# Two low-part subtractions per input projection of the first block move from VectorE to GpSimd

## The reference, cut to what matters

```python
hn = rms_norm(x, ln1)
proj = hn @ w_in                     # 1024 x 2824: the input projection
mq, mk, mv, sq, sk, sv, xqk, xv, xo, xi, xf = jnp.split(proj, idx, axis=-1)
mq, mk, sq, sk = (apply_rope(rms_norm(heads(a), g), cos, sin) for a, g in ...)
y_moba = moba_attention(mq, mk, mv)  # 6 heads, causal
qk = silu(causal_depthwise_conv(xqk, conv_w, conv_b))
h = mlstm_chunkwise(lq, lk, xv, i_pre, f_pre) * sigmoid(xo)   # 4 heads
y_swa = swa_attention(sq, sk, sv, sinks)   # 6 query heads, window 128
x = x + concat([y_moba, rms_norm(h), y_swa]) @ w_out
x = x + square(relu(rms_norm(x, ln2) @ w_up)) @ w_down
```

## Time and profile before

| | us |
|---|---|
| median of 3 runs | 1953.29 |
| lowest and highest | 1945.13, 1953.79 |
| the profiled execution, its own time | 1953.22 |
| its span | 1951.4 |
| PE busy in the span | 1851.1 (95%) |
| DVE busy | 1107.3 (57%) |
| ACT busy | 881.6 (45%) |
| GpSimd busy | 37.2 (2%) |
| the 274 splits on DVE (line 1013), sum and mean | 621.6, 2.276 |

### The profile page before, as it was taken

The page is one execution under the profiler, slowest core; times in us unless marked ns, Lnnn a source line. Parts: engine busy times, 40 slices in busy tenths (PEclk is TensorE's granted clock), DMA queues, the critical chain, the costliest instruction groups (busy, mean ns, idle before and its releaser), DMA issues.

```text
span 1951.4 us, 26268 instructions
## 1 busy us (share of the span) xinstructions
PE 1851.1 (95%) x11234; PEld 1593.2 (82%) x11234; DVE 1107.3 (57%) x1202; ACT 881.6 (45%) x1148; POOL 37.2 (2%) x29
## 2 busy tenths in 40 slices
PE   7898999989899999998999998998999999989998
PEld 6767999776799988776999986877999877868997
DVE  4865555485555555465655654556555654665554
ACT  5454444345444444434544543425444544344442
POOL 0000000000000000000000000000000000000000
PEclk9998999999899999999999998999999999998999
DMA  7463565645456574447555543366665652364552
GB/s 238 146 219 117 187 194 184 206 151 187 159 194 189 181 252 157 135 156 269 173 182 185 185 161 108 108 222 211 193 187 180 216 173 86 126 220 130 187 182 85
DMA packets 228235, 342.48 MB, mean 176 GB/s; under 512 B 9908, under 2 KB 118808, under 8 KB 227992
## 3 DMA queue, kind: packets, MB, share of 16 engines
q1 hardware_dynamic: 226928, 339.45, 53.6%
q10 hardware_dynamic: 1192, 1.36, 0.2%
HBM read 339.74 MB, written 1.05 MB: 175 GB/s over the span
## 4 chain that ended last, share of the span: by engine, by line
PE 89%; DVE 6%; ACT 3%; issue 1%; POOL 1%; ACTq 0%; DVEq 0%; POOLq 0%
PE PS L1604 16%; PE PS L1606 16%; PE PS L1605 16%; PE PS L1644 9%; PE PS L1645 9%; PE PS L1646 9%; PE PS L2032 2%; DVE LO L1013 1%; PE PS L1563 1%; PE PS L2013 1%; PE PS L2022 1%; PE PS L1941 1%; PE PS L1687 1%; POOL RS L565 1%; PE PS L2051 1%
## 5 line engine op out<-in xcount | busy, mean ns | idle before, releaser
L1013 DVE TENSOR_TENSOR LO<-RAW,HI 128x2048 fp32r<-128x2048 f32 (+1 forms) x274 | 621.6, 2276 | 447.5 <-ACT HI L584 446.9
L584 ACT CAST HI<-RAW 128x2048 fp32r<-128x2048 f32 (+1 forms) x274 | 516.7, 1894 | 321.3 <-PE PS L1606 257.3
L1644 PE MATMUL PS<-AH,HI 128*128 128x256 f32 x1424 | 408.4, 287 | 0.4 <-issue 0.4
L1645 PE MATMUL PS<-AL,HI 128*128 128x256 f32 x1424 | 405.8, 285 | 0.0
L1646 PE MATMUL PS<-AH,LO 128*128 128x256 f32 x1424 | 405.6, 285 | 0.0
L1604 PE MATMUL PS<-HI,AH 128*128 128x512 f32 (+2 forms) x848 | 318.1, 375 | 13.3 <-DVE MOD L1365 7.8
L1605 PE MATMUL PS<-LO,AH 128*128 128x512 f32 (+2 forms) x848 | 310.2, 366 | 0.0
L1606 PE MATMUL PS<-HI,AL 128*128 128x512 f32 (+2 forms) x848 | 310.0, 366 | 0.0
L1644 PEld LDWEIGHTS PS<-AH,HI 128*128 128x128 f32 x1424 | 276.6, 194 | 2.9 <-issue 2.3
L1645 PEld LDWEIGHTS PS<-AL,HI 128*128 128x128 f32 x1424 | 276.4, 194 | 1.6 <-issue 1.0
L1646 PEld LDWEIGHTS PS<-AH,LO 128*128 128x128 f32 x1424 | 276.2, 194 | 0.0
(11 more groups left out here) (244 smaller groups left out, 1640.2 us busy)
## 6 DMA issues: line engine op xcount, KB each, us to landing
RAW<-in_w_ff SPq DMA_DIRECT2D x96, 1024.0 KB, 5.4
RAW<-in_w_in SPq DMA_DIRECT2D x80, 1024.0 KB, 5.1
RAW<-in_w_mod SPq DMA_DIRECT2D x48, 1024.0 KB, 5.1
RAW<-in_w_up SPq DMA_DIRECT2D x32, 1024.0 KB, 5.5
RAW<-in_w_down SPq DMA_DIRECT2D x32, 1024.0 KB, 5.0
RAW<-in_w_o SPq DMA_DIRECT2D x12, 1024.0 KB, 6.1
RAW<-in_w_out SPq DMA_DIRECT2D x8, 1024.0 KB, 5.6
RAW<-in_w_attn_out SPq DMA_DIRECT2D x6, 1024.0 KB, 5.0
```

The lines of the kernel that those rows point to most:

```text
L584: return nc.scalar.copy(dst, src)
L1013: tt(LO[:, c % RAW_N, 0:n], RAW[:, c % RAW_N, 0:n], HI[:, NTH[c] % HL_N, 0:n].bitcast(F32), ALU.subtract).then_inc(s_lo, 1)
L1644: mm(o, wh, ah[:, j, :], start=j == 0, stop=False)
L1645: mm(o, wh, al[:, j, :], start=False, stop=False)
```

## The change

GpSimd takes over the subtraction of chunk 7 and of chunk 8 in both layers of the first block, four chunks in all, and counts them on a semaphore of its own, s_plo. In GpSimd's list they stand behind the second power of the layer (24 wide). DVE leaves these four out and numbers its own by LOW_NTH. `arrived(c)` waits for s_plo at these four chunks and for s_lo at the others.

```diff
+POOL_LOW = [k.c_in + j for k in LAYERS for j in (7, 8)]
+LOW_NTH = {c: i for i, c in enumerate(c for c in SPLITS if c not in POOL_LOW)}
...
+        s_plo = sem("chunk_split_by_pool")
...
                 for j, width in enumerate((2, 24, 2 * (NQK - 12), 8, 2)):
                     rsqrt(5 * l + j, width)
+                    if j == 1:
+                        for c in POOL_LOW[2 * l:2 * l + 2]:
+                            pool.wait_ge(s_hi, NTH[c] + 1)
+                            nc.gpsimd.tensor_tensor(LO[:, c % RAW_N, :], RAW[:, c % RAW_N, :],
+                                                    HI[:, NTH[c] % HL_N, :].bitcast(F32),
+                                                    ALU.subtract).then_inc(s_plo, 1)
...
             def ahead(c):
-                if c + SPLIT_LEAD in NTH:
+                if c + SPLIT_LEAD in LOW_NTH:
                     split(c + SPLIT_LEAD)
...
             def arrived(c):
-                pe.wait_ge(s_lo, NTH[c] + 1)
+                if c in POOL_LOW:
+                    pe.wait_ge(s_plo, POOL_LOW.index(c) + 1)
+                else:
+                    pe.wait_ge(s_lo, LOW_NTH[c] + 1)
```

## The result

The changed kernel takes 1976.05 us (median of 4 runs, 1966.39 to 1977.41) against 1953.54 of the kernel before (4 runs, 1945.13 to 1953.81): a ratio of 1.0115, 95% interval 1.0094 to 1.0135. It is slower by 22.5 us; 1978 was forecast, from 1970 to 1988. One of the four runs, at 1966.39, lies under that range. The profiled execution took 1977.2 us with a span of 1975.4, 24.0 more than before.

The account below looks back on a forecast made before the run. PE, busy 95% of the span, was taken as the bound, so its waits count. Per layer 11.6 us of late scores plus 0.9 for a second clock fall make 25.0 over two layers: 1953.2 + 25.0 = 1978 us, range 1970 to 1988.

Parts of the forecast that it names:

- The chain before the new work: Up to GpSimd's power, waits run through ACT's cast and DVE's split of chunk 9; power stays at 71.08 us.
- the value of 0 for the freed time: DVE's freed 4.6 us a layer gain nothing, since chunk 9's split waits for ACT's cast; upper end 4.6 us a layer.
- GpSimd's subtraction: One 128 x 2048 subtraction on GpSimd takes 4.9 us, taken as three passes at the pace of a memset.
- a sign that it is wrong: GpSimd's subtraction lasting under 2.5 or over 6 us would show the prediction wrong.
- PE's pause and start: PE idles 14.0 us ahead of chunk 7 in layer 0, waiting for GpSimd, and starts it at 80.25 us.
- The slow clock behind it: After the long pause PE runs chunk 7 partly at half clock, losing 2.6 us.
- The way to the scores: Chunk 11's split 1.99 us after its cast, mLSTM scores 3.49 us after the split: 94.05 against 82.43, 11.6 us late.
- The second fall of the clock: A later 3.1 us PE pause may lower the clock again, costing 0 to 2.6 us; a third, 0.9, was taken.
- The rival of engines in each other's way: DVE's scaling, 1.76 and 1.83 us, holds GpSimd's subtraction of chunk 7 by 3.6 us a layer: 1985 us; chance 0.20.
- what is added: Prediction's step on GpSimd's new work: wait for high parts free, each subtraction 4.9 us.
- The subtractions in time: Rival: GpSimd's subtractions are ready when PE needs them, nothing is lost, price 0, 1953 us; chance 0.06.

Follow-up runs that it names:

- e1: Changed kernel with nobody subtracting chunks 7 and 8; PE multiplies with the high part instead of the low: 1950.91 us against 1953.48 of before, ratio 0.9993.
- e5: Changed kernel with only chunk 7's subtraction on GpSimd behind the power, chunk 8 back on DVE: 1979.28 us in one run.
- e4: Kernel before, all splits on DVE, plus two GpSimd subtractions per layer behind the 24-wide power that nobody waits for: 1968.67 us, ratio 1.0084.
- e2: Changed kernel with GpSimd's two subtractions ahead of the 24-wide power instead of behind it: 1955.69 us, ratio 1.002.
- e8: e7 plus DVE's split of chunk 9 moved behind the sums of squares and that of chunk 10 behind the weighing: 1946.46 us, ratio 0.9969.
- e7: Kernel before, no GpSimd subtractions, DVE's split of chunk 11 moved behind its weighing of the mLSTM scores: 1948.42 us, ratio 0.9981.
- e9: e8 plus one wait holding DVE's split of chunk 9 until ACT's exponential of the mLSTM weights is done: 1943.00 us, ratio 0.9957 against before.
- e6: Changed kernel with 56 extra matmuls of 512 columns on PE ahead of chunk 7 in each layer: 1970.13 us, ratio 1.0089 against before.
- e3: Changed kernel with only chunk 8's subtraction on GpSimd behind the power, chunk 7 back on DVE: 1962.33 us in one run.

## Why the prediction was right, step by step

**The chain before the new work.** Right: the power starts at 71.08 in both profiles, DVE's idle time ahead of chunk 9 is 5.29 us, and e1 shows the value of 0 for the freed time directly.

**GpSimd's subtraction.** 4.9 us from the memsets, 4.49 for chunk 7 when it ran ahead of DVE. The 4497 ns of the Trainium skill (GPSIMD Engine Reference, the side-by-side cycle accounting) agree with this to a few nanoseconds; the estimate from three passes of a memset was 9% too high. Chunk 8's subtraction took 6.1 us, since DVE's first scaling came between. The prediction had named over 6 us as a sign that it is wrong, but meant GpSimd's own pace by it. PE reached chunk 8 only at 87.12, 1.3 us after it was ready, so this cost nothing.

**PE's pause and start.** 14.0 us forecast, 13.64 measured; the difference is the 0.4 us of the subtraction.

**The slow clock behind it.** 2.6 us forecast. Chunk 7 took 7.43 us (79.85 to 86.89 + 0.39) instead of 5.63 in layer 0, a loss of 1.8; in layer 1 it is 2.5, worked out from ACT's cast, 17.00 us behind the power where it is 16.30 in layer 0. The mean is 2.2.

**The way to the scores.** Cast to split 2.01 us (1.99 forecast), split to scores 3.48 (3.49). The scores are 10.4 us late in layer 0 and 11.2 in layer 1 (453.81 less 431.32 is 22.49 us behind the power, instead of 11.34); 11.6 was forecast.

**The second fall of the clock.** Forecast as possible, a pause of 3.1 us and a third of 2.6. The pause is 2.81 us and the clock fell behind it in both layers, for 1.6 us each (layer 0 goes from 10.4 to 12.1 us late, layer 1 from 11.2 to 12.7). A price of 0.9 was too small for this, and the overestimates above, nearly as large, cancelled it: 12.5 us a layer forecast, 12.1 and 12.7 measured. That the sum comes out so close is in part luck: in e5 the same pause of 2.81 us left the clock as it was in layer 0.

**The rest of the kernel.** The two layers give 24.8 us (12.1 and 12.7), and the profiled execution is 24.0 longer. In between, the delay moves with no edit near: it is 12.10 us at the third power of layer 0, 10.41 at the first of layer 1, 23.13 at the third of layer 1, 24.5 and 23.0 further on, 23.96 at the last. The medians of the runs differ by 22.5.

**The rival of engines in each other's way.** The collision happened, but the other way round: I had GpSimd held for DVE's 3.6 us and the result at 1985. In fact GpSimd went first and DVE was held, some 8.6 us over two instructions, and that was covered because DVE would have waited for chunk 11's cast anyway. The step that is missing is in "what is added": it looked for what could delay GpSimd and gave no price to what GpSimd does to DVE. e4 puts it at 7.8 us in layer 0, and with the subtractions in time for PE it is what makes the power late (e2). That the forecast of the time held without it is luck: with the lateness smaller by the 1.9 us that DVE still waited, the hold would have set the time. The rule in the Trainium skill (SBUF — State Buffer, "Who interferes with whom") says two things: that such pairs contend, and that whoever starts first keeps the other out for its whole instruction. The trace agrees with both, on two-input instructions in the changed kernel, and in e8 against GpSimd. I had used only the first. It does not agree for the power as the first one: DVE's two-input split at 72.49 took its usual 2.29 us inside the power of 71.08 to 75.25. There the measurement decides.

**The subtractions in time.** A price of 0 was too low: e2 is that case, and it is slower by 0.2% (0.03 to 0.37).

## What to carry to other kernels

Before work is moved to an idle engine, look up in that engine's list what it is queued behind and when that ends, and whether the time that is freed lies on the chain: here the place gave PE a pause of 13.6 us a layer, some 12 us late in the end, and the freed time was worth nothing (e1). A long GpSimd subtraction on SBUF has to be charged to DVE's work on SBUF as well, for as long as it lasts; that was so for every DVE instruction seen beside one here (two tensors from SBUF, or a scaling of one). What the profile offered was a reordering with no engine changed: an instruction that is on the chain, and whose result is wanted late, goes behind the work that is wanted first (e7 to e9; e9 is 0.43% faster than before).

## What the runs showed of the hardware

GpSimd's subtractions and DVE took turns by whole instructions: 4.49 us of GpSimd's made 6.04 of DVE's 1.76. But GpSimd's power of 24 elements let DVE's splits run beside it at their full 2.29 us if they started 1.4 us (changed kernel) or 1.75 us (e9) after it, and was itself held, 6.14 instead of 4.17 us, by a split that had started 0.17 us before it. This fits a power that needs the way to its operands only at its start; that it is the reading and nothing else was not tested.

A pause of 2.4 to 2.9 us in PE brought the clock down at some times and not at others, at the same length. Ahead of the transposes of QK these profiles have ten such pauses. The clock was about 0.5 for the 3 to 4 us behind six of them (changed kernel 2.81 and 2.83, e5 2.80, e6 2.41, e9 2.81 and 2.83) and stayed full behind four (e3 2.77, e5 2.81, e6 2.42, e8 2.82). Each fall cost some 1.6 us.

Part of the scatter between runs goes with PE's clock. Between the powers at 1587.20 and 1753.84 us, late in the second block, the code is the same in both kernels, and PE does the same 770 matmuls. The first row is of before, the second of e1:

```profile
1587.20:1753.84 166.64, 153.83 (x770) 119.44 (x768) 97.11 (x102) 67.96 (x105) 3.53 (x1) 0.95 0.46 151
```

```profile
1587.05:1749.44 162.39, 149.57 (x770) 116.24 (x768) 97.02 (x102) 67.92 (x105) 3.53 (x2) 0.99 0.47 155
```

e1 gained 4.2 us there with no edit (0.15 us ahead at the first power, 4.40 at the second) at a clock of 0.99 instead of 0.95, and e2 gained 4.3. In the series of e9, single executions of before went from 1945.10 at a mean clock of 0.977 to 1954.16 at 0.974. A comparison by single profiles must therefore be made inside the stretch that was edited.
